# Values of the first layer: from TensorE transposes to sixteen block transposes on VectorE and a split on GpSimd

## The reference, cut to what matters

```
h = x * (1.0 + sc) + sh
q, k, v, z = jnp.split(h @ w_in[l], 4, axis=-1)
s = concatenate([q k_window * scale + bias, q k_context * scale])
p = softmax(s)
y = p_window @ v_window + p_context @ v_context
out = (y * silu(z)) @ w_out[l]
x = layer_norm(ALPHA * x + (1 + g) * out) * ln_g + ln_b
```

## Time and profile before

| | |
|---|---|
| median of 3 runs | 1776.35 us (1776.16 to 1777.1) |
| the profiled execution's own time | 1775.98 us |
| its span in the trace | 1774.0 us |
| PE busy | 98% |
| DVE, ACT, POOL busy | 72%, 51%, 21% |
| mean granted TensorE clock | 0.996 |

### The profile page before, as it was taken

How to read it: one execution, slowest core, us unless ns; L and a number is a source line. 1 busy time by engine, 2 the same in 40 slices (tenths; PEclk the granted TensorE clock), 3 DMA queues, 4 the chain that set the end, 5 groups by cost and what they waited for, 6 DMA issues and landing times. The chain is left out here.

```text
span 1774.0 us, 30535 instructions
## 1 busy us (share of the span) xinstructions
PE 1739.0 (98%) x10205; PEld 1508.1 (85%) x10205; DVE 1280.0 (72%) x2317; ACT 905.5 (51%) x1610; POOL 368.2 (21%) x413
## 2 busy tenths in 40 slices
PE   7999999999999999999999999999999999999998
PEld 3898989898988898878878889888888888898886
DVE  6687787878787878747878585766858484857658
ACT  4665655555555555640137465464647374654500
POOL 2221212121111112348331010101000010103951
PEclk9999999999999999999999999999999999999999
DMA  9615151424141423316330010202020100102243
GB/s 360 144 46 131 43 127 48 116 55 114 57 118 53 115 57 96 103 57 229 131 88 35 26 48 12 62 12 53 9 62 12 43 31 28 46 12 72 93 160 119
DMA packets 130775, 142.89 MB, mean 81 GB/s; under 512 B 89602, under 2 KB 97954, under 8 KB 130596
## 3 DMA queue, kind: packets, MB, share of 16 engines
q1 hardware_dynamic: 111524, 112.26, 21.0%
q0 software_dynamic: 16464, 20.52, 5.4%
q10 hardware_dynamic: 2736, 9.44, 1.4%
HBM read 110.73 MB, written 17.79 MB: 72 GB/s over the span
## 5 line engine op out<-in xcount | busy, mean ns | idle before, releaser
L678 PE MATMUL acc<-h_hi,w_hi 128*128 128x512 f32 (+1 forms) x1408 | 520.3, 370 | 4.8 <-DVE h_lo L599 3.6
L678 PE MATMUL acc<-h_hi,w_lo 128*128 128x512 f32 (+1 forms) x1408 | 509.3, 362 | 0.0
L678 PE MATMUL acc<-h_lo,w_hi 128*128 128x512 f32 (+1 forms) x1408 | 508.9, 361 | 0.0
L678 PEld LDWEIGHTS acc<-h_hi,w_hi 128*128 128x128 f32 x1408 | 266.4, 189 | 43.3 <-DVE h_lo L599 4.5
L678 PEld LDWEIGHTS acc<-h_hi,w_lo 128*128 128x128 f32 x1408 | 266.0, 189 | 41.8
L678 PEld LDWEIGHTS acc<-h_lo,w_hi 128*128 128x128 f32 x1408 | 266.6, 189 | 34.8
L1893 DVE TENSOR_REDUCE stats<-acc 128x1 f32<-128x1280 f32 x128 | 189.6, 1487 | 39.0 <-PE acc L2000 37.5
L1809 ACT ACTIVATE far_pt<-acc 128x512 f32<-128x512 f32 (+1 forms) x192 | 101.3, 528 | 162.2 <-PE acc L2009 158.7
L1802 ACT ACTIVATE far_prob<-acc,stats 128x1280 f32<-128x1280 f32 x128 | 170.2, 1330 | 24.4 <-DVE stats L1893 22.7
L2000 PE MATMUL acc<-k_dup,q_stack 128*128 128x512 f32 (+1 forms) x768 | 176.8, 367 | 1.7 <-ACT far_prob L1802 0.6
L973 POOL TENSOR_TENSOR far_prob<-far_prob,far_rope 128x512 f32<-128x512 f32 x32 | 41.3, 1291 | 636.5 <-DVE far_prob L962 636.5
(11 more groups left out here) (231 smaller groups left out, 2912.3 us busy)
## 6 DMA issues: line engine op xcount, KB each, us to landing
w_raw<-in_w_in SPq DMA_DIRECT2D x64, 512.0 KB, 3.4
near_late_slots<-in_w_mod SPq DMA_DIRECT2D x64, 256.0 KB, 2.7
w_raw<-in_w_out SPq DMA_DIRECT2D x16, 512.0 KB, 3.3
w_raw<-y_t POOLq DMA_DIRECT2D x14, 448.0 KB, 5.5
near_values<-near_values POOLq DMA_DIRECT2D x16, 384.0 KB, 6.7
token_cols<-in_x_cols SPq DMA_DIRECT2D x8, 640.0 KB, 8.3
far_v<-far_v_blocks SPq DMA_DIRECT2D x128, 40.0 KB, 2.0
y_t<-y SPq DMA_DIRECT2D x7, 640.0 KB, 3.0
```

Of the source, the lines that this page charges most:

```text
L678: mm = nc.tensor.matmul(m.bank(self.bank_of(j, c), w), wt[:, b % 2, k, :], ht[:, k, t0:t0 + w], start=(k == 0 and i == 0), stop=(k == KT - ...
```

## The change

The ten transposes on TensorE, ScalarE's high parts and VectorE's low parts of the values are gone. In their place VectorE transposes blocks of 32x32 within `k_raw` and writes them to `v_rows`, which is the first 1280 columns of `near.prob`. One instruction takes one quarter q of the channels (32 partitions) and, of each of the ten token tiles, the quarter r of 32 tokens: 320 columns in, 320 out, into partitions 32r to 32r + 31. Sixteen such instructions turn all values. They stand in four groups of four (one for each q) between the Q splits. GpSimd waits for eight of them (head 0), copies to the high part and subtracts for the low part (128 partitions, 10x64 elements each), and does the same for head 1 after all sixteen. Only then does it move the values. The factor 0.5 is applied as V is copied from PSUM.

ScalarE waits for the finished split before the first exponential of the chunk, since that writes `near.prob`.

```
+        self.v_rows = self.prob[:, :, :].rearrange("p b n -> p (b n)")[:, 0:TOK].rearrange("p (t n) -> p t n", n=P)
...
-    def values_hi(self, act, c, n):
-        act.wait_ge(self.v_turned, CREDIT + c * self.NV + (n + 1))
+    def turn_v_blocks(self, v, c, q):
+
+        if q == 0:
+            v.wait_ge(self.evac, CREDIT + c * self.evacs + 3)
+        blocks = self.m.k_raw[q * BLOCK:(q + 1) * BLOCK, 0:TOK].rearrange("p (t r n) -> p r t n", r=QUADS, n=BLOCK)
+        for r in range(QUADS):
+            self.nc.vector.transpose(self.near.v_rows[r * BLOCK:(r + 1) * BLOCK, :, q * BLOCK:(q + 1) * BLOCK],
+                                     blocks[:, r]).then_inc(self.v_turned, 1)
...
+    def split_values(self, pool, c):
         for h in range(2):
...
+            src, hi, lo = self.value_parts(h)
+            pool.wait_ge(self.v_turned, CREDIT + c * self.NV + 2 * QUADS * (h + 1))
+            self.nc.gpsimd.tensor_copy(hi, src).then_inc(self.v_hi, 1)
+            pool.wait_ge(self.v_hi, CREDIT + c * 2 + h + 1)
+            self.nc.gpsimd.tensor_tensor(lo, src, f(hi), ALU.subtract).then_inc(self.v_ready, 1)
 
     def move_values(self, pool, c, shift):
 
-        pool.wait_ge(self.v_ready, CREDIT + c * 2 * self.NV + 4)
+        pool.wait_ge(self.v_ready, CREDIT + c * 2 + 2)
...
     def pe_part(self, pe, c, ring_free, gate_bank_free, late, first):
 
-        ring_free(pe, 0)
-        self.turn_v(pe, c, 0)
-        ring_free(pe, 1)
-        self.turn_v(pe, c, 1)
...
         late.reduce(pe, c, 7)
-        self.turn_v(pe, c, 2)
+        ring_free(pe, 0)
+        ring_free(pe, 1)
...
     def dve_part(self, v, c, last, late):
         self.split_lo_part(v, self.nc.vector, c, 2)
-        self.values_lo(v, c, 0)
-        self.values_lo(v, c, 1)
...
-        self.values_lo(v, c, 2)
         self.split_lo_part(v, self.nc.vector, c, 3)
+        self.turn_v_blocks(v, c, 0)
         late.sum(v, c, 1)
         for j in range(6, self.cum[2]):
             self.split_x_lo(v, c, j)
+            self.turn_v_blocks(v, c, j - 5)
             late.sum(v, c, j - 4)
...
                 for c in range(NCH):
+                    p.split_values(pool, c)
                     for shift in range(len(SHIFTS)):
                         p.move_values(pool, c, shift)
...
                     p.act_part(act, c, lambda e: e.wait_ge(y_ready, CREDIT + c * COLS), last, late)
+                    act.wait_ge(p.v_ready, CREDIT + c * 2 + 2)
```

More of the change, by code:

```diff
@@ L621, in __init__ @@
         lat_only = l == DEPTH - 1
+        self.v_scale = 1.0 if lat_only else 0.5
         self.q_groups = 2 if lat_only else 3
@@ L681, in product_part @@
             mm.then_inc(self.proj, 1)
-    def turn_v(self, pe, c, n):
-        pe.wait_ge(self.evac, CREDIT + c * self.evacs + (self.v_turns[n][0] + 1))
-        if n >= 2:
-            pe.wait_ge(self.v_ready, CREDIT + c * self.v_parts * self.NV + self.v_parts * (n - 1))
-        for i, t0 in enumerate(self.v_turns[n][1]):
-            mm = self.nc.tensor.transpose(self.m.psum[:, self.turn_bank(n), i * P:(i + 1) * P], self.m.k_raw[:, t0:t0 + P],
-                                          self.m.ident[:, :])
-        mm.then_inc(self.v_turned, 1)
     def evacuate(self, act, c, j):
@@ L701, in evacuate @@
         self.nc.scalar.activation(dst[:, t0:t0 + w], self.m.bank(self.bank_of(j, c), w), ACT.Copy,
-                                  scale=SCALE if b == 2 else 1.0).then_inc(self.evac, 1)
+                                  scale=(self.v_scale, 1.0, SCALE)[b]).then_inc(self.evac, 1)
     def duplicate_k(self, act, c, h):
@@ L736, in __init__ @@
         self.v_moved = [stack.enter_context(nc.semaphore(f"p0_v_moved{shift}")) for shift in range(len(SHIFTS))]
-        self.v_turns = [(g, range(t0, t0 + w, P)) for g, (t0, w) in enumerate(GROUPS)]
-        self.NV = len(self.v_turns)
-        self.evacs, self.v_parts = 3, 2
+        self.NV = QUADS * QUADS
+        self.evacs = 3
         self.splits = 2 * (self.cum[2] - 3)
@@ L756, in bank_free @@
             pe.wait_ge(self.x_lo, CREDIT + c * self.splits + 2 * (j - 6))
-    def turn_bank(self, n):
-        return 5 - n % 2
-    def turned_values(self, n, h):
-        count = len(self.v_turns[n][1])
-        src = self.m.bank(self.turn_bank(n), count * P).rearrange("p (t h n) -> p h t n", h=2, n=HD)[:, h]
-        dst = self.near.values[:, 4 * n:4 * n + count, h, :].rearrange("p t (part n) -> p part t n", part=2)
-        return src, dst[:, h], dst[:, 1 - h]
-    def values_hi(self, act, c, n):
-        act.wait_ge(self.v_turned, CREDIT + c * self.NV + (n + 1))
-        for h in range(2):
-            src, hi, lo = self.turned_values(n, h)
-            self.nc.scalar.activation(hi, src, ACT.Copy, scale=0.5).then_inc(self.v_hi, 1)
@@ L774, in values_lo @@
-    def values_lo(self, v, c, n):
-        for h in range(2):
-            v.wait_ge(self.v_hi, CREDIT + c * 2 * self.NV + (2 * n + 2))
-            src, hi, lo = self.turned_values(n, h)
-            self.nc.vector.scalar_tensor_tensor(lo, src, 0.5, f(hi), ALU.mult, ALU.subtract).then_inc(self.v_ready, 1)
+    def turn_v_blocks(self, v, c, q):
[5 more added lines that the diff above has]
+                                     blocks[:, r]).then_inc(self.v_turned, 1)
@@ new lines, in value_parts @@
+    def value_parts(self, h):
+        parts = self.near.values[:, 0:TOK_TILES, h, :]
+        return self.near.v_rows[:, :, h * HD:(h + 1) * HD], parts[:, :, h * HD:(h + 1) * HD], parts[:, :, (1 - h) * HD:(2 - h) * HD]
+    def split_values(self, pool, c):
+        for h in range(2):
+            src, hi, lo = self.value_parts(h)
[3 more added lines that the diff above has]
+            self.nc.gpsimd.tensor_tensor(lo, src, f(hi), ALU.subtract).then_inc(self.v_ready, 1)
@@ L855, in act_part @@
         self.split_hi_part(act, c, 2)
-        self.values_hi(act, c, 0)
-        self.values_hi(act, c, 1)
         self.split_x_hi(act, c, 3)
@@ L861, in act_part @@
         late.take_row(act, c, 7)
-        self.values_hi(act, c, 2)
         self.split_hi_part(act, c, 3)
@@ L901, in __init__ @@
         self.rot_shuffled, self.rot_scaled, self.dve = (self.sem("rot_" + n) for n in ("shuffled", "scaled", "dve"))
-        self.v_turns = [(g, range(t0, t0 + w, P)) for g, (t0, w) in enumerate(GROUPS)]
-        self.NV = len(self.v_turns)
+        self.NV = len(GROUPS)
         self.turned_by = [1, 2, 3]
@@ L1608, in values @@
                             pe.wait_ge(p.gate_done, CREDIT + c * p.q_groups + 1)
-                            pe.wait_ge(p.v_ready, CREDIT + c * 2 * p.NV + 2 * p.NV)
+                            pe.wait_ge(p.v_ready, CREDIT + c * 2 + 2)
                         if u.local and u.shift is not None and j == 0 and u.head == 0:
```

## The result

The changed kernel takes **1838.57 us** (median of 6, 1836.71 to 1841.95) beside 1776.78 (median of 6) of the kernel before on the same chip: the ratio is 1.0352, with an interval of 1.0341 to 1.0362. The direction was forecast, the size was not: 1810 was said, and 1838.6 lies above the range (1786 to 1833). The profiled execution took 1838.05 us, its span is 1836.3 against 1774.0.

The account below looks back on a forecast made before the run. TensorE's own list was taken to bound a chunk, with 3.8 us of room on VectorE. Chunk 0's 5.2, six middle chunks' 19.8 and the last chunk's 8.5 made 33.5 us on 1775.98: 1809.5, said as 1810; range 1786 to 1833.

Parts of the forecast that it names:

- Sixteen transposes cost 8.0 us: VectorE in each chunk: sixteen new transposes at 0.50 us each add 8.0 us, with bounds of 6.2 and 11.5 us.
- The second kind of neighbour: VectorE: instructions changing quarter do not overlap, like K splits, 0.03 us more than one lasts from start to start.
- 1.74 us removed, 3.8 us of idle time filled: VectorE before the first row maximum: the values' low parts save 1.74 us, and about 3.8 us of idle time can be filled.
- The two engines stop one another for 2.75 us: VectorE ahead of the row maximum: GpSimd's copies and a subtraction stop sums and weight split, 2.75 us, bounds 0 and 4.5.
- 2.0 us of slack: Second scores in a middle chunk: the exponentials they need could come 2.0 us later and nobody would wait.
- 3.3: Each middle chunk grows by 3.3 us: 0.55 from VectorE's later list plus 2.75 from the two engines' collisions.
- A small wait ahead of the first scores: TensorE before the first scores: they come at about 354.4 instead of 354.2, a wait inside the larger one.
- a rival of its own: TensorE's clock falls behind its wait ahead of the second scores, 17 us more in seven chunks, 1827; chance 0.12.
- my case: The main forecast: slower, 1810 us, own range 1800 to 1819, with TensorE idle some 4 us a chunk; chance 0.42.
- Chunk 0, +5.2: First chunk: row maximum 6.4 us later, scores at 93.3 against 88.19, so 5.2 us longer.
- The last chunk, +8.5: Last chunk: GpSimd's queue delays the output projection's start and ScalarE's wait for weight slice 2, 8.5 us longer.
- Rival 2: VectorE's transposes cost 0.72 us each, every chunk 3.5 us longer, 28 us in all, 1838; chance 0.15.

Follow-up runs that it names:

- transposes tiny: Changed kernel with each of the sixteen transposes turning one 32x32 block instead of ten, GpSimd's split kept the same size; 1788.5 us (ratio 1.0070).
- split tiny: Changed kernel with GpSimd splitting one column of each head instead of 640 from chunk 1 on; 1801.0 us (ratio 1.0139).
- sums first: Changed kernel with each pair of sums put ahead of the group of transposes instead of behind it; 1812.0 us (ratio 1.0199).
- own quarter: Changed kernel with four transposes in a row reading and writing the same quarter of the partitions, values not put in their places; 1821.8 us.
- the last kernel: Changed kernel with VectorE's list reordered, y's transfer early in the last chunk, and GpSimd splitting the next weights after the first row maximum; 1772.98 us (ratio 0.9986).

## Why the prediction was wrong

One table puts the kernels together: first row maximum after the start of a middle chunk, length of the chunk, and the granted clock over whole middle chunks.

| kernel | row maximum | chunk | clock |
|---|---|---|---|
| transposes tiny | 25.8 | 91.3 | 1.00 |
| split tiny | 26.85 | 92.4 | 1.00 |
| sums first | 27.7 | 93.4 or 95.0 | 1.00 or 0.98 |
| own quarter | 28.8 | 94.3 to 97.2 | 0.96 to 1.00 |
| changed kernel | 30.55 | 97.4 to 98.9 | 0.97 to 0.98 |

At full clock the chunk grows by 3.0 us (91.3 to 94.3) while the row maximum moves by 3.1: one for one. By that line the changed kernel's chunk would be 91.3 + 4.8 = 96.1 us. TensorE's own times give the same: at full clock it is busy for 90.0 us of a chunk, and in chunk 3 it waits 2.26, 3.48 and 0.31 us. The fall of the clock adds 1.3 to 2.8 us to it.

Step by step, in a middle chunk:

- *Sixteen transposes cost 8.0 us.* 8.5: 0.53 each, not 0.50. The second kind of neighbour (K splits, held) was the right row, its duration was read too low: the new instruction lasts 0.502 us, where I put it between the two full-width rows at 0.47.
- *1.74 us removed, 3.8 us of idle time filled.* Right: 8.5 - 1.74 + 3.76 - 6.65 leaves 3.87 us filled.
- *The two engines stop one another for 2.75 us.* 3.76. The mechanism and both places were right, down to the instruction; for head 0 I let the pair of sums lose only the copy, as I put the copy between the two sums and the subtraction beside the Q split. The copy went first instead (the first sum took 1.30 us), so that the subtraction fell between the sums (the second took 2.07), and each pair lost both, 1.88 us. The weight split behind it, which I had as the one stopped for head 1, was not touched (1.21 us at 385.04).
- *2.0 us of slack.* 1.85: with the row maximum 1.85 us later than before (transposes tiny) the chunk was not longer.
- So these terms give 6.65 - 1.85 = 4.8 us where the prediction had 3.3: 1.5 us a chunk, 9 in six.
- *A small wait ahead of the first scores.* It was 2.26 us. It does not lengthen the chunk by itself, as the second one is later, but TensorE now stood twice within 11 us.
- **The step that failed: the clock was a rival of its own, with 0.12, and not a part of my case.** My case had TensorE stand for nearly 4 us a chunk, which was that rival's own condition; the two could not exclude each other. The argument against it, that TensorE came out of dense matmuls here, did not hold: the clock fell in every chunk of the changed kernel, in chunks 1 and 5 behind 2.3 us of standing already, in the others behind 3.5. The six chunks grew by 41.6 us; 6 x 4.8 = 28.8 of it is delay, and 12.8, 2.1 a chunk, is the clock. The rival had 2.5 us a chunk. Added to my sum it would have given 1827, inside the range. Neither kind of error alone leaves the range: without the 12.8 us the measured time would be near 1826, and my sum with only these 12.8 us more is near 1823. Both together do.
- *Chunk 0, +5.2.* It was +9.1. The row maximum moved by 10.3 us instead of 6.4: hardly any idle time was filled. The first sum now waits 3.31 us for its transfer and starts at 67.69; before, the values' low parts stood ahead of it, and it started at 66.24 without a wait. So what was removed there gained nothing, and the 2.6 us of idle time that I meant to fill further on were spent here. The transfer was issued 0.3 us later than before (62.2 against 61.9, queue of SyncE); why it took some 5.5 us from there was not traced.
- *The last chunk, +8.5.* +11.4: the mechanism (GpSimd's queue, slice 2, ScalarE) was right, and moving one transfer took 6.6 us of it. The low part of the first output weights began 12.0 us later within the chunk, not 8.4 (52.8 against 40.8 us after its start); the transfer of y alone kept GpSimd 8.46 us, where 6.1 was assumed. The clock fell here too (0.83 from 780 to 790 us). Of the 11.4 us, 4.8 stayed when the transfer was moved, and their cause is not shown.

The shortfall of the sum is 62.3 - 33.5 = 28.8 us of span: 9 from sizes in the middle chunks, 12.8 from the clock, 4 from chunk 0, 3 from the last one. Rival 2 would give nearly the measured time, 1838, but for a wrong reason: it asked for 0.72 us a transpose, and no run shows more than 0.53.

Left open: why chunks of the same waits sometimes keep their clock (in the kernel with transposes inside one quarter it stayed at 1.00 with waits of 0.95 and 3.04 us in chunk 1, and fell with 0.98 and 3.06 in chunk 2), and which engine goes first when both reach for SBUF within 0.05 us.

## What to carry to other kernels

If a forecast contains new idle time on TensorE, the price of the clock behind it belongs in the same sum and not in a rival with a chance of its own. When work moves to VectorE and GpSimd together, list for each of GpSimd's operations what VectorE runs beside it: sums with two SBUF inputs were stopped here, Q splits that read PSUM and one SBUF tensor were not, and the same work in another order was worth 50 us. Find by a tiny version of each new piece how far the first dependent result may slip before the stage is longer than it was (here 1.85 us); beyond that point every microsecond counts, and short of it the slip may still eat what the change was to save (91.3 us a chunk with the row maximum at 25.8 us, 90.2 in the last kernel with 24.2).

## What was not expected of the hardware

- A change of quarter holds a VectorE instruction on the reading side as much as on the writing side: 0.53 us from start to start with either changed, 0.42 with none.
- The stop goes both ways: a copy of 0.72 us on GpSimd took 1.77 behind a weight split of VectorE that had begun 0.03 us earlier, and VectorE was not slowed.
- With equal waits of 1.15 and 1.87 us in 93 to 95 us of work, the clock fell in four chunks and not in two others, for 1.6 us.
